# Mixture of experts in a hybrid decoder step: every low weight part is made by VectorE

## The chip, the cores and the metric

The kernel runs on one core of a Trainium2 chip. The metric is the device time of one execution in microseconds (us); the time given is the median of three runs. The engines go by the profile's names: PE is TensorE (PEld its weight loads), DVE is VectorE, ACT is ScalarE, POOL is GpSimd, SP is SyncE, which here only issues DMAs.

## The reference

One inference step of a two-layer decoder for 256 prompt positions and 64 sample positions (320 tokens of width 1024). Layer 0 is pooling and forgetting attention, cross-attention and a dense SwiGLU; layer 1 is a convolution module and stick-breaking attention, cross-attention and a mixture of eight experts. Only the last part is touched here:

```
logits = (h @ w_router).astype(f32) + b_router
top_val, top_idx = lax.top_k(logits, 2)
gates = softmax(top_val)              # spread over the 8 experts: combine
for e in range(8):
    out = out + combine[..., e:e+1] * swiglu(h, we_gate[e], we_up[e], we_down[e])
# swiglu(h, g, u, d) = (silu(h @ g) * (h @ u)) @ d,  1024 -> 3584 -> 1024, all fp32
```

## The kernel before

Each expert handles up to 128 gathered tokens. Its weights stream from HBM in 42 pieces of 128x2048 fp32 (1 MB). Seven column blocks (STAGES) of 512 hidden channels give the products (0, j) gate, (1, j) up and (2, j) down, j from 0 to 6. PRODUCTS (line 61) is the order of their use: (0,0), (1,0), then for j from 1 to 6 the three (0,j), (1,j), (2,j-1), and last (2,6). Each product takes two pieces, q = 0 and q = 1.

TensorE multiplies in a rounded fp32 form, so that each fp32 operand is split in a high and a low part, and three products of parts are summed (split_product, line 1072): high by high, low tokens by high weight, high tokens by low weight. A piece costs 12 matmuls of 128x512. For each piece:

- SP loads it into one of seven raw buffers (PRING = 7) as soon as TensorE has finished the piece seven places earlier (line 1380).
- ACT copies it to its high part (weights_hi, line 2147; the copy helper records line 1672).
- The low part, raw minus high, is written over the raw buffer. VectorE makes it for 35 of the 42 pieces (weights_lo, line 2858); GpSimd for the seven with m = 2 and q = 1, the second piece of every down product (POOLED, line 65; pooled, line 1601). Each has a semaphore of its own, and lo_parts (line 393) names the one and the count that TensorE waits for before a piece.

Each engine runs its own queue in order. VectorE's is written in expert (line 2867): at product b it makes the low parts of product b + 2, and beside that hidden(j), which multiplies the gate by the up result (line 2874), hidden_lo(j), the low part of the transposed hidden block (line 2879), and tokens_lo (line 2864), the low part of the next expert's tokens. At a product (0, j) the order is: low parts of (2, j-1), then hidden_lo(j-1). At (1, 6) it is: low parts of (2, 6), hidden(6), tokens_lo of the next expert; then follow the first piece of the next expert, hidden_lo(6), and the second piece.

TensorE transposes the hidden block j (line 1140) after product (0, j+1), multiplies (1, j+1), and then needs hidden_lo(j) for (2, j). At an expert's end it transposes the next expert's tokens (line 1118).

The results of the first seven experts go to scratch memory, the last one from expert 6 by a DMA that SP issues before piece 12 of expert 7 (line 1368). In the last expert, GpSimd's queue fetches them back per token in six indirect DMAs (outputs_back, line 1629), the first after that store has landed, those from the third on after VectorE has used up the buffer two back. VectorE adds them to x in combine(0) to combine(5) (line 2849), at the products b = 7, 9, 11, 13, 15, 17 of the last expert. In GpSimd's queue these fetches stand between its low parts: two pieces, fetches 0 and 1, two pieces, fetches 2 and 3, one piece, fetches 4 and 5, two pieces.

Of the kernel before, what the change touches and what calls it, by code (L numbers as in the profile page):

```python
# [18 lines left out]
F32 = mybir.dt.float32  # L19
# [3 lines left out]
ALU = mybir.AluOpType  # L23
# [16 lines left out]
NE = 8  # L40
# [21 lines left out]
PIECES = [(m, j, q) for m, j in PRODUCTS for q in range(2)]  # L62
NPIECE = len(PIECES)
PIECE = SLOT // 2
POOLED = [i for i, (m, j, q) in enumerate(PIECES) if m == 2 and q == 1]
PRING = 7
CAP = P
ROUNDS = -(-T // CAP)
# [109 lines left out]
def decoder_step(nc, a, o, scratch, known):  # L178

    ctx = ExitStack()  # L180
    with ctx:
# [16 lines left out]
        def sem(name):  # L198
            return ctx.enter_context(nc.semaphore(name))
# [142 lines left out]
        def pieces_of(small, large):  # L342
            return [(small if s < RING else large)[:, (s % RING if s < RING else s - RING) * SLOT + q * PIECE:][:, 0:PIECE]
                    for s in (0, 1, 3, 4, 5, 6, 2) for q in range(2)]

        raw = pieces_of(small_ring, big)[:PRING]
        low = pieces_of(ring_r, big_r)[:PRING]
        high = pieces_of(ring_r, big_r)[PRING:]
# [14 lines left out]
        full = [sem(f"bank{b}_full") for b in range(8)]  # L363
        free = [sem(f"bank{b}_free") for b in range(8)]
        raw_full = [sem(f"raw{s}_full") for s in range(PRING)]
        moe_hi, moe_lo, moe_lo_pool, moe_used, moe_xhi, moe_hThi = (sem("moe_" + n) for n in (
            "weights_hi", "weights_lo", "weights_lo_pool", "weights_used", "tokens_hi", "hiddenT_hi"))
        slot_full = [sem(f"slot{s}_full") for s in range(XSLOTS)]
        knat_full = [sem(f"knat{s}_full") for s in range(4)]
        ffn_gate, ffn_up, ffn_silu, ffn_h, ffn_down, ffn_whi, ffn_wlo, ffn_hsplit, ffn_hlo_ready = (  # L370
# [15 lines left out]
        def primed(s, value):  # L386

            return s, value + 1
# [3 lines left out]

        def lo_parts(n, i):

            mine = i % NPIECE in POOLED
            rank = sum((p_ in POOLED) == mine for p_ in range(i % NPIECE))
            per = len(POOLED) if mine else NPIECE - len(POOLED)
            return moe_lo_pool if mine else moe_lo, n * per + (i // NPIECE * per + rank + 1)

        def used(n, m, j):  # L400

# [37 lines left out]

        stream = list(w_stream())  # L440
        place = {key: (n % RING, n // RING) for n, (key, _) in enumerate(stream)}

        FBLK = DFF // 256
        n0 = next(n for n, (key, _) in enumerate(stream) if key[1] == 1)
        extra = [0, 2 * (FBLK // 2 + 1), 2 * (FBLK // 2)]

# [3 lines left out]
        def slot_of(key):  # L450

            s, use = place[key]
            n = next(m for m, (k, _) in enumerate(stream) if k == key)
            return s, use + 1 + (extra[s] if n >= n0 else 0)
# [37 lines left out]
        def _(pe):  # L492
# [581 lines left out]
            def split_product(n, m, j, out, x_hi_lo, chunks, between=None):  # L1074


                for q in range(2):
                    i = 2 * PRODUCTS.index((m, j)) + q
                    pe.wait_ge(*lo_parts(n, i))
                    w = [t[i % PRING].rearrange("p (k n) -> p k n", k=chunks) for t in (high, low)]  # L1080
                    for k in range(chunks):
                        kk = q * chunks + k
                        for xa, wa in ((0, 0), (1, 0), (0, 1)):
                            for dst, wcols in out(w[wa][:, k, :]):
                                ins = mm(dst, x_hi_lo[xa][kk], wcols,  # L1085
                                         start=(m < 2 or j == 0) and kk == 0 and (xa, wa) == (0, 0),
                                         stop=(m < 2 or j == STAGES - 1) and kk == 2 * chunks - 1 and wa == 1)
                    ins.then_inc(moe_used, 1)
                    if q == 0 and between is not None:
                        between()  # L1090
# [320 lines left out]
        def _(pool):  # L1411
            tt, ts = nc.gpsimd.tensor_tensor, nc.gpsimd.tensor_scalar
# [116 lines left out]
            r = NSAMP  # L1529
# [65 lines left out]
                        pool.dma_start(new_rows("sb_v", t), v[0:ROWS[t], t, :]).then_inc(*sets("v_out", 1, by=16))  # L1595
                    state_stores(1, "conv", CBUF, "state_conv")

            def pooled(n, pieces):
                for i in pieces:
                    pool.wait_ge(moe_hi, n * NPIECE + (i + 1))  # L1600
                    tt(low[i % PRING], raw[i % PRING], high[i % PRING].bitcast(F32), ALU.subtract) \  # L1601
                        .then_inc(moe_lo_pool, 1)

            def send_rows(r):

                pool.wait_ge(moe_rows_at, r + 1)
                if type(r) is int:
                    pool.wait_ge(moe_fill, 16)
                else:
                    pool.wait_ge(moe_rows_in, r * 16 * (NE - 1))  # L1610
                    pool.sem_inc(pool_passed, 1)
                for i in range(6):
                    t = i // 2
                    pool.indirect_dma_start(
                        out=scratch["tokens"], out_offset=bass.IndirectOffsetOnAxis(ap=row_at[0:ROWS[t], i:i + 1], axis=0),
                        in_=h[0:ROWS[t], t, :], in_offset=None, bounds_check=NE * CAP - 1, oob_is_err=False) \
                        .then_inc(moe_sent, 16)

            def outputs_back(r, i):

                t = i // 2
                if i == 0:
                    pool.wait_ge(*primed(moe_y_out, (r + 1) * 16 * (NE - 1)))
                    pool.wait_ge(*primed(moe_gathered, (r + 1) * 2 * NE))
                if i >= 2:
                    pool.wait_ge(*primed(moe_combined, r * 6 + (i - 1)))
                if type(r) is not int:
                    pool.sem_inc(pool_passed, 1)
                pool.indirect_dma_start(
                    out=moe_back[i % 2][0:ROWS[t], :], out_offset=None, in_=scratch["outputs"],  # L1630
                    in_offset=bass.IndirectOffsetOnAxis(ap=row_at[0:ROWS[t], i:i + 1], axis=0),
                    bounds_check=(NE - 1) * CAP - 1, oob_is_err=False).then_inc(moe_back_in[i % 2], 16)

            def expert_round(r):
                send_rows(r)
                with pool.Fori(0, NE - 1) as e:
                    pooled(e + r * NE, POOLED)
                n = r * NE + (NE - 1)
                pooled(n, POOLED[0:2])
                outputs_back(r, 0)  # L1640
                outputs_back(r, 1)
                pooled(n, POOLED[2:4])
                outputs_back(r, 2)
                outputs_back(r, 3)
                pooled(n, POOLED[4:5])
                outputs_back(r, 4)
                outputs_back(r, 5)
                pooled(n, POOLED[5:])

            expert_round(0)  # L1650
            pool.wait_ge(*at("cmax"))
            most = pool.value_load(cmax_i[0:1, 0:1])
            with pool.If(most > CAP):
                with pool.Fori(1, ROUNDS) as r:
                    expert_round(r)
# [556 lines left out]
        def _(dve):  # L2212
# [347 lines left out]
            for t in range(TILES):  # L2560
                r = ROWS[t]
                ins = V.tensor_tensor(lf_y[0:r, t, :], bank[b][0:r, 16 * t:16 * t + 8], b_f[0:r, :], ALU.add)
            step(ins)
            for t in range(TILES):
                r = ROWS[t]
# [191 lines left out]
            for t in range(TILES):  # L2757
                r = ROWS[t]
# [24 lines left out]
            for t in range(TILES):  # L2783
                r = ROWS[t]
# [67 lines left out]
            def weights_lo(n, b, parts=(0, 1)):  # L2852

                for i in (2 * b + q for q in parts):
                    if i % NPIECE in POOLED:
                        continue
                    dve.wait_ge(moe_hi, n * NPIECE + (i + 1))
                    V.tensor_tensor(low[i % PRING], raw[i % PRING], high[i % PRING].bitcast(F32), ALU.subtract) \  # L2858
                        .then_inc(moe_lo, 1)
# [107 lines left out]
```

## Time and profile before

| | us |
|---|---|
| median of three runs | 2050.26 (2046.18 to 2051.13) |
| the profiled execution | 2052.65 |
| its span in the profile | 2050.8 |
| before the experts' first product | about 1064 |
| experts and end | 1064 to 2051 |

The profile is of one execution. Times in the views count from the span's start; what lies around the span is 1.85 us. A timeline row has the start, the duration, the engine, the line, the operation with output and inputs, the count, and in brackets how long the engine stood idle before it and what released it. PE's matmuls are pipelined: a row's duration is longer than the step from one start to the next.

### The profile page before, as it was taken

To read this page: it belongs to the slowest core of one execution; us is meant where nothing else is said; L and a number is where in the kernel's file an instruction comes from. 1 tells how busy PE (TensorE), PEld (TensorE's weight loads), DVE (VectorE), ACT (ScalarE), POOL (GpSimd) and SP (SyncE) were. 2 spreads that over 40 slices of the span, in tenths; PEclk is the share of its full clock that TensorE was granted. 3 is DMA by queue.
4 is the path that set the end of the run, shared out by engine and by line. 5 is a ranking of instruction groups with operands and counts; after the bars stand their busy time and mean duration, and the time that the engine had idled before them with its cause. 6 is when DMAs were issued, how large, how long until landed. Compare 5 with 4: busy or idle time off the path is not lost.

```text
span 2050.8 us, 23715 instructions
## 1 busy us (share of the span) xinstructions
PE 1851.5 (90%) x8761; PEld 1449.0 (71%) x8761; DVE 1266.6 (62%) x1170; ACT 1064.8 (52%) x1052; POOL 460.6 (22%) x225
## 2 busy tenths in 40 slices
PE   6998978899998845697789999999999999999987
PEld 5785343799987834434378888888888888888865
DVE  5543032544435996203158888787878878788875
ACT  4333122423224315602137777777777777777663
POOL 4220010000003740001013322322332232233243
PEclk9999999899998976899969999999999999999999
DMA  9443206454444520421629999999999999999984
GB/s 302 137 157 107 94 29 207 144 162 126 150 142 166 192 81 26 149 82 41 215 96 381 373 374 388 363 393 361 390 374 377 387 364 394 363 389 372 374 334 151
DMA packets 236737, 497.88 MB, mean 243 GB/s; under 512 B 14994, under 2 KB 46882, under 8 KB 236653
## 3 DMA queue, kind: packets, MB, share of 16 engines
q1 hardware_dynamic: 223629, 479.11, 65.2%
q0 software_dynamic: 4544, 13.57, 1.9%
q10 hardware_dynamic: 8496, 4.33, 0.7%
q8 instruction: 39, 0.64, 0.1%
q14 instruction: 29, 0.24, 0.0%
HBM read 480.46 MB, written 17.35 MB: 243 GB/s over the span
## 4 chain that ended last, share of the span: by engine, by line
PE 78%; DVE 11%; issue 4%; ACT 3%; DMA 2%; POOL 1%; SPq 1%; DVEq 0%; ACTq 0%; POOLq 0%
PE bank L1085 40%; PE bank L532 8%; PE bank L960 8%; DVE big L2718 4%; PE bank L569 4%; PE bank L980 3%; PE bank L567 2%; DVE small_ring_r L2858 1%; PE bank L596 1%; PE bank L1140 1%; ACT big_r L1672 1%; PE bank L720 1%; PE bank L1106 1%; DMA small_ring<-in_w_ck 1%; PE bank L522 1%
## 5 line engine op out<-in xcount | busy, mean ns | idle before, releaser
L1672 ACT ACTIVATE big_r<-small_ring 128x2048 fp32r<-128x2048 f32 x240 | 456.0, 1915 | 139.3 <-DMA small_ring<-in_we_up 45.7
L2858 DVE TENSOR_TENSOR small_ring_r<-small_ring,big_r 128x2048 fp32r<-128x2048 f32 x168 | 441.2, 2656 | 44.5 <-ACT big_r L1672 44.4
L1085 PE MATMUL bank<-big_r,hT_r 128*128 128x512 f32 x1024 | 385.9, 395 | 10.3 <-DVE small_ring_r L2858 8.7
L1085 PE MATMUL bank<-small_ring_r,hT_r 128*128 128x512 f32 x768 | 302.3, 394 | 0.0
L1085 PE MATMUL bank<-big_r,kM_r 128*128 128x512 f32 x704 | 275.8, 392 | 0.0
L1085 PEld LDWEIGHTS bank<-big_r,hT_r 128*128 128x128 f32 x1024 | 193.3, 189 | 50.8 <-issue 11.2
L1672 ACT ACTIVATE small_ring_r<-big 128x2048 fp32r<-128x2048 f32 x96 | 183.3, 1916 | 52.2 <-DMA big<-in_we_up 28.0
L1601 POOL TENSOR_TENSOR small_ring_r<-small_ring,big_r 128x2048 fp32r<-128x2048 f32 x24 | 124.6, 5193 | 374.5 <-ACT big_r L1672 374.5
L2858 DVE TENSOR_TENSOR big_r<-big,small_ring_r 128x2048 fp32r<-128x2048 f32 x72 | 176.1, 2461 | 26.9 <-ACT small_ring_r L1672 26.9
L1601 POOL TENSOR_TENSOR big_r<-big,small_ring_r 128x2048 fp32r<-128x2048 f32 x24 | 123.4, 5141 | 197.8 <-ACT small_ring_r L1672 197.8
L1085 PEld LDWEIGHTS bank<-small_ring_r,hT_r 128*128 128x128 f32 x768 | 145.1, 189 | 30.2
L1085 PEld LDWEIGHTS bank<-big_r,kM_r 128*128 128x128 f32 x704 | 133.2, 189 | 26.8
L1672 ACT ACTIVATE big_r<-big 128x2048 fp32r<-128x2048 f32 x59 | 113.2, 1918 | 41.6 <-DMA big<-in_we_up 12.8
L532 PE MATMUL bank<-small_ring,h 128*128 128x512 f32 (+1 forms) x288 | 128.6, 604 | 2.9 <-ACT h L1672 2.1
L960 PE MATMUL bank<-hT_r,big_r 128*128 128x320 f32 x352 | 110.1, 313 | 5.2 <-DVE small_ring_r L2636 5.2
L1085 PE MATMUL bank<-big_r,PT_r 128*128 128x512 f32 x416 | 112.9, 390 | 0.4 <-DVE PT_r L2879 0.4
L2347 DVE TENSOR_TENSOR x<-x,bank 128x512 f32<-128x512 f32 (+1 forms) x24 | 16.4, 685 | 155.8 <-PE bank L532 155.8
L960 PE MATMUL bank<-hT_r,small_ring_r 128*128 128x320 f32 x352 | 109.9, 312 | 0.0
L2858 DVE TENSOR_TENSOR big_r<-big,big_r 128x2048 fp32r<-128x2048 f32 x40 | 91.4, 2285 | 27.9 <-ACT big_r L1672 27.9
L532 PEld LDWEIGHTS bank<-small_ring,h 128*128 128x128 f32 (+1 forms) x288 | 49.3, 176 | 80.0 <-issue 80.0
L1085 PE MATMUL bank<-small_ring_r,PT_r 128*128 128x512 f32 x352 | 98.9, 392 | 3.4 <-DVE PT_r L2879 3.4
L1085 PE MATMUL bank<-big_r,kN_r 128*128 128x512 f32 x352 | 96.0, 395 | 0.0
(398 smaller groups left out, 3252.7 us busy)
## 6 DMA issues: line engine op xcount, KB each, us to landing
small_ring<-in_we_gate SPq DMA_DIRECT2D x80, 1024.0 KB, 5.9
small_ring<-in_we_up SPq DMA_DIRECT2D x64, 1024.0 KB, 5.4
big<-in_we_down SPq DMA_DIRECT2D x64, 1024.0 KB, 5.8
big<-in_we_up SPq DMA_DIRECT2D x48, 1024.0 KB, 6.6
small_ring<-in_we_down SPq DMA_DIRECT2D x48, 1024.0 KB, 5.7
big<-in_we_gate SPq DMA_DIRECT2D x32, 1024.0 KB, 5.2
small_ring<-in_w_gate SPq DMA_DIRECT2D x11, 1024.0 KB, 5.5
small_ring<-in_w_up SPq DMA_DIRECT2D x11, 1024.0 KB, 8.0
```

The costliest lines, as they stand in the source:

```text
L522: ins = tr(bank[b][:, k * P:k * P + ROWS[t]], src[0:ROWS[t], t, (4 * kh + k) * P:(4 * kh + k + 1) * P], ident[0:ROWS[t], 0:ROWS[t]])
L532: ins = mm(bank[b][0:ROWS[t], 0:cols], xT[:, k, t0:t0 + ROWS[t]], w[:, k, col0:col0 + cols], start=k == 0, stop=k == nk - 1)
L567: ins = mm(bank[b][:, 0:T], w[wa][:, k, i * P:(i + 1) * P], x[xa][kk], start=first, stop=last)
L569: ins = mm(bank[b][0:ROWS[i], :], x[xa][kk][:, i * P:i * P + ROWS[i]], w[wa][:, k, :], start=first, stop=last)
L596: ins = tr(bank[b][:, c * P:(c + 1) * P], knat[:, j % 4, c * P:(c + 1) * P], ident)
L960: ins = mm(bank[bk][:, 0:T], w[wa][:, m, k, f2 * P:(f2 + 1) * P], ffn_x[:, k, :] if xa == 0 else ffn_xlo[k // 4][:, k % 4, :], start=k == ...
L980: ins = mm(out[0:ROWS[t], :], (ffn_hhi, ffn_plo)[xa][f2][:, t * P:t * P + ROWS[t]], w[wa][:, f2, wc], start=first and (xa, wa) == (0, 0), ...
L1085: ins = mm(dst, x_hi_lo[xa][kk], wcols, start=(m < 2 or j == 0) and kk == 0 and (xa, wa) == (0, 0), stop=(m < 2 or j == STAGES - 1) and kk ...
L1601: tt(low[i % PRING], raw[i % PRING], high[i % PRING].bitcast(F32), ALU.subtract) \
L1672: return A(out, in_, ACT.Copy)
L2718: ins = V.scalar_tensor_tensor(accp, inp, cw[:, j, c:c + 1], accp, ALU.mult, ALU.add)
L2858: V.tensor_tensor(low[i % PRING], raw[i % PRING], high[i % PRING].bitcast(F32), ALU.subtract) \
```

## The change

POOLED and GpSimd's pooled are removed, together with the semaphore moe_lo_pool. VectorE's weights_lo no longer leaves out the seven pieces, so that it makes all 42 of an expert in the order of PRODUCTS; lo_parts counts them all on one semaphore. GpSimd keeps the sending of the token rows at the start and the six fetches of the last expert, now one behind the other with nothing between. What the pieces are split into, the order of the products, the DMAs of SP and ACT's queue stay.

```diff
-POOLED = [i for i, (m, j, q) in enumerate(PIECES) if m == 2 and q == 1]
...
         def lo_parts(n, i):
-            mine = i % NPIECE in POOLED
-            rank = sum((p_ in POOLED) == mine for p_ in range(i % NPIECE))
-            per = len(POOLED) if mine else NPIECE - len(POOLED)
-            return moe_lo_pool if mine else moe_lo, n * per + (i // NPIECE * per + rank + 1)
+            return moe_lo, n * NPIECE + (i + 1)
...
-            def pooled(n, pieces):
-                for i in pieces:
-                    pool.wait_ge(moe_hi, n * NPIECE + (i + 1))
-                    tt(low[i % PRING], raw[i % PRING], high[i % PRING].bitcast(F32), ALU.subtract) \
-                        .then_inc(moe_lo_pool, 1)
...
             def expert_round(r):
                 send_rows(r)
-                with pool.Fori(0, NE - 1) as e:
-                    pooled(e + r * NE, POOLED)
-                n = r * NE + (NE - 1)
-                pooled(n, POOLED[0:2])
-                outputs_back(r, 0)
-                outputs_back(r, 1)
-                pooled(n, POOLED[2:4])
-                outputs_back(r, 2)
-                outputs_back(r, 3)
-                pooled(n, POOLED[4:5])
-                outputs_back(r, 4)
-                outputs_back(r, 5)
-                pooled(n, POOLED[5:])
+                for i in range(6):
+                    outputs_back(r, i)
...
             def weights_lo(n, b, parts=(0, 1)):
                 for i in (2 * b + q for q in parts):
-                    if i % NPIECE in POOLED:
-                        continue
                     dve.wait_ge(moe_hi, n * NPIECE + (i + 1))
                     V.tensor_tensor(low[i % PRING], raw[i % PRING], high[i % PRING].bitcast(F32), ALU.subtract) \
                         .then_inc(moe_lo, 1)
```

## Rows read from the trace of the kernel before

**Rows 1.** Windows: length, busy (count) of PE, PEld, DVE, ACT, POOL, clock, DMA share, GB/s.

```profile
1776.57:1895.98 119.41, 118.84 (x540) 98.14 (x541) 99.23 (x52) 91.34 (x63) 35.60 (x7) 1.00 1.02 378
1895.98:2028.36 132.38, 121.85 (x536) 98.81 (x536) 106.86 (x58) 83.14 (x56) 51.43 (x13) 0.97 0.88 325
...
1960.00:1970.00 10.00, 10.00 (x47) 7.98 (x46) 10.00 (x6) 7.11 (x5) 0.84 (x1) 1.00 1.04 398
```

**Rows 2.** Waits from 1240 to 1950 us: total us, times, longest us.

```profile
PEld bank L1085 <- DVE small_ring_r L2858: 5.3, 6, 1.1
...
PE bank L1085 <- DVE PT_r L2879: 2.8, 6, 0.7
```

**Rows 3.** Timeline of POOL, DVE and PE at the last expert's long stall.

```profile
1971.96 6.11 POOL L1601 TENSOR_TENSOR big_r<-big,small_ring_r 128x2048 fp32r<-128x2048 f32 x1 [11.13 <-ACT small_ring_r L1672]
1978.22 1.01 POOL L1629 DMA_INDIRECT gain<-scratch_outputs,row_at  x1
...
1985.41 1.28 DVE L2849 SCALAR_TENSOR_TENSOR x<-gain,rt,x 128x1024 f32<-128x1024 f32 x1 [11.22 <-DMA gain<-scratch_outputs,row_at]
...
1989.04 0.76 PE L1085 MATMUL bank<-big_r,hT_r 128*128 128x512 f32 x1 [7.90 <-DVE small_ring_r L2858]
1989.60 0.63 PE L1085 MATMUL bank<-big_r,kM_r 128*128 128x512 f32 x1
```

**Rows 4.** VectorE's low-part line, largest group: minimum, median, maximum in ns.

```profile
L2858 DVE TENSOR_TENSOR small_ring_r<-small_ring,big_r x168: 2273/2281/6085, 1047.5 to 2014.4; 128x2048 fp32r<-128x2048 f32 x168
```

**Rows 5.** Timeline of POOL, DVE and PE about one product (2, 0).

```profile
1320.56 6.33 POOL L1601 TENSOR_TENSOR small_ring_r<-small_ring,big_r 128x2048 fp32r<-128x2048 f32 x1 [24.04 <-ACT big_r L1672]
...
1320.11 2.29 DVE L2858 TENSOR_TENSOR small_ring_r<-small_ring,big_r 128x2048 fp32r<-128x2048 f32 x1
1322.61 0.69 DVE L2879 TENSOR_TENSOR PT_r<-bank,PT_r 128x512 fp32r<-128x512 f32 x1 [0.22 <-ACT PT_r L1672]
1324.42 4.62 DVE L2858 TENSOR_TENSOR small_ring_r<-small_ring,big_r 128x2048 fp32r<-128x2048 f32 x1 [1.11 <-ACT big_r L1672]
...
1327.18 1.07 PE L1085 MATMUL bank<-big_r,PT_r 128*128 128x512 f32 x4
```

**Rows 6.** Timeline of POOL, DVE, ACT and PE at an expert's end.

```profile
1768.31 5.38 POOL L1601 TENSOR_TENSOR big_r<-big,small_ring_r 128x2048 fp32r<-128x2048 f32 x1 [1.24 <-ACT small_ring_r L1672]
...
1766.46 2.76 DVE L2858 TENSOR_TENSOR big_r<-big,small_ring_r 128x2048 fp32r<-128x2048 f32 x1 [1.11 <-ACT small_ring_r L1672]
1769.60 0.69 DVE L2874 TENSOR_TENSOR qz<-Pr,bank 128x512 f32<-128x512 f32 x1 [0.38 <-PE bank L1085]
1770.51 1.29 DVE L2864 TENSOR_TENSOR kM_r<-bank,hT_r 128x512 fp32r<-128x512 f32 x2 [0.22 <-ACT hT_r L1672]
1772.80 3.04 DVE L2858 TENSOR_TENSOR small_ring_r<-small_ring,big_r 128x2048 fp32r<-128x2048 f32 x1 [1.01 <-ACT big_r L1672]
1775.77 0.68 DVE L2879 TENSOR_TENSOR PT_r<-bank,PT_r 128x512 fp32r<-128x512 f32 x1
1776.37 6.68 DVE L2858 TENSOR_TENSOR small_ring_r<-small_ring,big_r 128x2048 fp32r<-128x2048 f32 x3
...
1764.52 3.71 ACT L1672 ACTIVATE small_ring_r<-big 128x2048 fp32r<-128x2048 f32 x2
...
1772.88 0.60 PE L1140 MATMUL bank<-consts,qz 128*128 128x128 f32 x4
1776.57 1.19 PE L1085 MATMUL bank<-small_ring_r,PT_r 128*128 128x512 f32 x4 [0.32 <-DVE PT_r L2879]
```

**Rows 7.** Timeline of SP and DVE: the store before the fetches, the first combine.

```profile
1915.83 0.42 SPq L1368 DMA_DIRECT2D scratch_outputs<-qz  x1
...
1952.86 1.28 DVE L2849 SCALAR_TENSOR_TENSOR x<-gain,rt,x 128x1024 f32<-128x1024 f32 x1 [0.35 <-DMA gain<-scratch_outputs,row_at]
```

**Rows 8.** DMA from 1900 us on: a queue's packets, MB, share; issues, KB, us to landing.

```profile
q0 software_dynamic: 736, 2.24, 4.0%
...
scratch_outputs<-qz SPq DMA_DIRECT2D x1, 512.0 KB, 9.8
```

More of the change, by code:

```diff
@@ L365, in decoder_step @@
         raw_full = [sem(f"raw{s}_full") for s in range(PRING)]
-        moe_hi, moe_lo, moe_lo_pool, moe_used, moe_xhi, moe_hThi = (sem("moe_" + n) for n in (
-            "weights_hi", "weights_lo", "weights_lo_pool", "weights_used", "tokens_hi", "hiddenT_hi"))
+        moe_hi, moe_lo, moe_used, moe_xhi, moe_hThi = (sem("moe_" + n) for n in (
+            "weights_hi", "weights_lo", "weights_used", "tokens_hi", "hiddenT_hi"))
         slot_full = [sem(f"slot{s}_full") for s in range(XSLOTS)]
```

## The prediction

> **What bounds the kernel now.** I read the windows by stage first, then the waits, then the timelines where PE stands still.
>
> From 1064 us on the kernel is eight equal experts. One of them takes 119.41 us, and PE is busy for 118.84 of them, with a DMA share of 1.02 and 378 GB/s [rows 1]. The waits say that PE is the bound and not the DMAs: over six experts PE's matmuls waited 2.8 us for hidden_lo, and its weight loads 5.3 us for the low part made just before it, both once per expert, at its end [rows 2]. VectorE is busy for 99.23 us of the 119.41, POOL for 35.60.
>
> The last expert is the exception. It has four matmuls fewer (536 to 540) and takes 132.38 us [rows 1]: 13 us more than its neighbour. The reader is to see why [rows 3]. POOL made a low part at 1971.96, for which it had waited 11.13 us, and only behind it issued the third fetch, at 1978.22. VectorE's combine(2) needs that fetch and stood idle for 11.22 us until 1985.41; the low parts behind combine(2) came late, and PE stood idle for 7.90 us until 1989.04. The next matmul comes 0.56 us later [rows 3], where the mean step of an expert is 119.41 / 540 = 0.22, and the granted clock of this expert is 0.97 on the mean, of the one before 1.00 [rows 1]: after the stall PE ran for a while on the lower of its levels, 1.2 GHz.
>
> **The change part by part.**
>
> VectorE's added work. A low part on VectorE takes 2.28 us in the median but up to 6.09 [rows 4]. The long ones stand beside POOL's: POOL's piece of 1320.56 ends at 1326.89, and VectorE's piece of 1324.42 ends at 1329.04, 2.15 later; POOL's piece of 1768.31 ends at 1773.69, and VectorE's of 1772.80 ends at 1775.84, again 2.15 later [rows 5, 6]. So VectorE's instruction with two operands in SBUF waits until POOL's is done, and loses that with the change. In a row of three undisturbed ones the step is (6.68 - 2.28) / 2 = 2.20 us [rows 6]. An expert then costs VectorE 42 x 2.20 = 92.4 us, and the 16 short instructions (7 hidden, 7 hidden_lo, 2 tokens_lo) 16 x 0.6 = 9.6: 102 us of the 119.4, hardly more than the 99.23 of now. That is the lower end. The upper is that a piece keeps its present mean for some other reason: (99.23 - 9.6) / 36 = 2.49 us [rows 1], and 42 x 2.49 + 9.6 = 114 us. Either end is under 119.4; I take 102, since the median is the undisturbed piece.
>
> Where the seven pieces stand. Six per expert come before hidden_lo(j-1). The tightest is the first: VectorE's piece of 1320.11 is done, by the step, at 1322.3; the added one (its high part is there, POOL began on it at 1320.56) at 1324.5, and hidden_lo, now at 1322.61, at 1325.2. PE needs it at 1327.18 [rows 5]: 2.0 us to spare, and the piece after it, now ending at 1329.04, is done at 1327.4. They fall into VectorE's waits for ACT. So the steady stage stays PE's, and I cost these six at nothing; without this cover each us past the spare would cost 8 us over the eight experts.
>
> The seventh stands at the expert's end, before hidden(6) and tokens_lo. High parts come from ACT at 1766.4 and 1768.23; the low parts are then made at 1766.46 and 1768.7, hidden(6) at 1770.9 in place of 1769.60, tokens_lo at 1771.5 to 1772.8, just ahead of PE's transposes at 1772.88. The next expert's first piece starts at 1772.80 as now, but is done at 1775.0 in place of 1775.84, and hidden_lo(6) at 1775.7 in place of 1776.45: the 0.32 us that PE waited before 1776.57 are gone, with some 0.1 us to spare [rows 6]. At best the seven boundaries give back what the weight loads waited, 7 x 5.3 / 6 = 6.2 us; by the matmuls' wait it is 7 x 2.8 / 6 = 3.3 us [rows 2]; at worst hidden(6) comes late to the transposes and costs as much. I take half of the middle one, 1.6 us, since the margins are of 0.1 us.
>
> POOL's queue in the last expert. The fetches no longer stand behind low parts. The store of expert 6 is issued at 1915.83 and lands 9.8 us later [rows 7, 8], so that fetches 0 and 1 can leave at 1926 in place of 1943. Combine(0), which now starts at 1952.86 after a wait of 0.35 [rows 7], no longer waits. Fetch 2 waits for combine(0) alone, so it leaves at about 1954 and is there some 7 us later (1978.22 to 1985.41 now [rows 3]), long before combine(2), which began its wait at 1985.41 - 11.22 = 1974.2 [rows 3]. The 11.22 us of VectorE and PE's 7.90 go, and the slow matmuls after it. What is late next is nothing on VectorE: the six combines of 1.28 us [rows 7] add under 8 us in the last expert, and selecting the gates (line 2838) some 4: 114 of 119. The last expert should take what the one before takes, less the four transposes it lacks (0.4): 119.0 us. Gain 132.38 - 119.0 = 13.4 us. The boundaries are counted above.
>
> What is left against this is the DMAs. With 42 x 1.05 = 44.0 MB of weights, the store's 0.5 and the fetches' 2.24 MB [rows 8] the last expert moves 46.8 MB, against 45.1 in one before it (weights, one store, one fetch of tokens of 0.5 each). In the best window, 398 GB/s flowed [rows 1]: 46.8 MB / 398 = 117.6 us, just inside 119.0. The fetches now come right behind the store. I take off 1 us, with 0 and 5 as bounds.
>
> Sum: 13.4 + 1.6 - 1 = 14.0 us. From the profiled execution 2052.65 - 14.0 = 2038.6 us. That execution lies 2.4 us above the median of 2050.26, so I forecast 2036 us.
>
> **The rivals.**
>
> The DMAs are the bound as soon as the stall is gone. For it: a share of 1.02 in the steady stage, at 378 GB/s [rows 1]. Then the last expert takes 46.8 MB / 378 = 123.8 us, the boundaries give nothing, and the gain is 8.6 us: 2042 us. Against it: windows at 398, and PE, not the loads, has the last word. In its strongest form the last expert's 132.38 us are already those of its loads, and only the 1.6 us of the boundaries come: 2048.7 us; against that stand its 398 GB/s in a window, more than a whole stall-free expert needs, and a rate over all of it of 325 [rows 1], which is what a queue that waits for PE gives. A rule of the Trainium skill speaks for this form: SBUF — State Buffer, section "Summary: rules for kernel authors", says to reckon with about 358 GB/s between HBM and SBUF, by which 46.8 MB would take an estimated 131 us and the time would stay near 2049 us. By that rule the 378 GB/s over a whole expert [rows 1] could not be; the trace disagrees on this core.
>
> The stall only moves: the third fetch or a low part is late for another reason in the last expert, and only the shorter pieces help. For it: VectorE has 5 us to spare there, and no order of the fetches without POOL's pieces is in the trace. It leaves 8 of the 13.4 us standing: 2050.3 - 14 + 8 = 2044 us.
>
> Slower: the added piece delays hidden_lo. Its place is the product (2, j) in all experts. The spare there is 2.0 us, in the one place worked out above; if all 48 (six per expert) are like it, a piece of more than 4.2 us makes PE wait, and one of 4.5 us eats the whole gain (48 x 0.3 = 14 us). At 4.62 us, which VectorE's piece of 1324.42 took [rows 5], the loss is 48 x 0.4 = 19 us: 2036 + 19 = 2055 us. Against it: the long durations are those beside POOL, of which none are left.
>
> That the change doesn't do what it says can hardly be: no other work of POOL remains in the stage but the fetches.
>
> **How the numbers follow.** Forecast 0.70; DMAs at 378 GB/s 0.14, and in their strongest form 0.04; the stall moves 0.07; slower 0.05. Faster by over 0.3% means under 2044.1 us, about what a measurement here can tell: the forecast, the DMAs at 378, and a part of the moved stall, 0.86. Within 0.3%: 0.08. Slower 0.06. The range goes from 2028 (the middle gain at all boundaries, no loss to DMAs, 2033, and the 5 us by which the runs before differ) to 2047, which takes in the DMA rival and the moved stall.
>
> **What would show it.** POOL's busy time in an expert falls from 35.60 to nothing; VectorE's low parts all lie near 2.28 us, 42 an expert, and its busy time in an expert is about 102 us. PE takes some 119 us for each expert, the last one too, with no wait near 7.90 us and a clock of 1.00 throughout; fetch 0 leaves before 1930, and no combine waits for a fetch. The forecast is wrong if low parts over 3 us remain with POOL at rest, if PE waits for hidden_lo in the middle of an expert, or if PE waits for loads in the last one.

## The result

The changed kernel takes 2037.35 us, the median of eight runs (2030.33 to 2040.26); the kernel before, measured beside it, 2050.73 (2046.18 to 2056.99). The ratio is 0.9928, with an interval of 0.9909 to 0.9947: faster by 0.7%. Two later sets with the same kernel gave 0.9957 (0.9941 to 0.9974) and 0.9956 (0.9938 to 0.9974). By the medians the three sets gained 13.4, 8.8 and 9.3 us, so that the gain is some 10 us and the first set is the most favourable of the three.

The profiled executions can't simply be subtracted. The new one has a span of 2032.2 us, 18.6 less than before, but 8.5 us of that lie ahead of the experts, in code that is the same: the first product starts at 1055.84 in place of 1064.35 us. Over all the profiles of this study it starts between 1053 and 1064 us, whatever the kernel. So I take the time from the first product to the span's end: 986.4 us before, 976.4 after, 10.1 less. (Before stands on one profile, the change on three.) The first products, before and after:

```profile
1064.35 0.79 PE L1085 MATMUL bank<-big_r,hT_r 128*128 128x512 f32 x1 [1.59 <-DVE kM_r L2864]
```

```profile
1055.84 0.79 PE L1081 MATMUL bank<-big_r,hT_r 128*128 128x512 f32 x1 [1.59 <-DVE kM_r L2841]
```

The windows of the kernel after, of an inner expert and of the last, with the columns as in [rows 1]: length, busy us and count of PE, PEld, DVE, ACT and POOL, clock, DMA share, GB/s. (They begin 0.1 to 0.2 us behind the product's first matmul, which shortens a length by up to 0.1.)

```profile
1766.00:1884.50 118.50, 118.50 (x541) 98.12 (x541) 104.55 (x59) 91.25 (x63) 0.00 (x0) 1.00 1.03 381
1884.50:2009.88 125.38, 119.30 (x537) 97.26 (x536) 108.79 (x65) 83.78 (x56) 11.51 (x6) 1.00 0.94 345
```

An inner expert has fallen from 119.41 to 118.50, and PE is busy all the time. The last one has fallen from 132.38 to 125.38 us, and is still 7 us longer than its neighbour. POOL is at rest but for the fetches.

VectorE's low parts (minimum, median, maximum in ns; before: [rows 4]):

```profile
L2835 DVE TENSOR_TENSOR small_ring_r<-small_ring,big_r x192: 2274/2291/2296, 1039.0 to 1994.9; 128x2048 fp32r<-128x2048 f32 x192
L2835 DVE TENSOR_TENSOR big_r<-big,small_ring_r x96: 2276/2293/2296, 1064.0 to 2003.7; 128x2048 fp32r<-128x2048 f32 x96
```

All 336 lie between 2.27 and 2.30 us; before, the longest took 6.09.

About the product (2, 0), where [rows 5] gave the spare, the timeline of DVE and PE has

```profile
1309.83 4.49 DVE L2835 TENSOR_TENSOR small_ring_r<-small_ring,big_r 128x2048 fp32r<-128x2048 f32 x2
1314.23 0.68 DVE L2856 TENSOR_TENSOR PT_r<-bank,PT_r 128x512 fp32r<-128x512 f32 x1
1314.84 2.28 DVE L2835 TENSOR_TENSOR small_ring_r<-small_ring,big_r 128x2048 fp32r<-128x2048 f32 x1
...
1316.92 1.07 PE L1081 MATMUL bank<-big_r,PT_r 128*128 128x512 f32 x4
```

The added piece is the second of the x2. hidden_lo is done at 1314.91, 2.0 us before PE's need, and the next piece follows without the long wait for POOL. At the expert's end, where [rows 6] stood before:

```profile
1756.19 4.49 DVE L2835 TENSOR_TENSOR big_r<-big,small_ring_r 128x2048 fp32r<-128x2048 f32 x2 [1.11 <-ACT small_ring_r L1651]
1760.60 0.68 DVE L2851 TENSOR_TENSOR qz<-Pr,bank 128x512 f32<-128x512 f32 x1
1761.20 1.28 DVE L2841 TENSOR_TENSOR kM_r<-bank,hT_r 128x512 fp32r<-128x512 f32 x2
1762.53 2.29 DVE L2835 TENSOR_TENSOR small_ring_r<-small_ring,big_r 128x2048 fp32r<-128x2048 f32 x1
1764.74 0.69 DVE L2856 TENSOR_TENSOR PT_r<-bank,PT_r 128x512 fp32r<-128x512 f32 x1
...
1762.62 0.60 PE L1136 MATMUL bank<-consts,qz 128*128 128x128 f32 x4
...
1765.82 1.07 PE L1081 MATMUL bank<-small_ring_r,PT_r 128*128 128x512 f32 x4
```

tokens_lo ends at 1762.48, 0.14 us before the transposes at 1762.62; hidden_lo(6) ends at 1765.43, and PE goes on at 1765.82 with no idle time. Here the margins of a tenth or two held.

In the last expert PE still waits, in three rows of the waits from 1884.5 us on (total, times, longest):

```profile
PE bank L1136 <- DVE qz L2851: 3.2, 1, 3.2
PE bank L1081 <- DVE kN_r L2856: 1.6, 2, 1.0
PE bank L1081 <- DVE PT_r L2856: 1.4, 1, 1.4
```

All name VectorE, but what made VectorE late is mostly not its own. The chain that ended last goes, for the earliest of them (PE at 1930.64, behind hidden_lo in kN_r), back to a load that took 10.76 us to land, issued between the first two fetches:

```profile
1914.96 10.76 DMA small_ring<-in_we_down
1925.74 1.93 ACT big_r L1651
1927.69 2.29 DVE small_ring_r L2835
1929.99 0.61 DVE kN_r L2856
...
1930.64 11.22 PE bank L1081 x48
```

For the longest, the 3.2 us before the transposes at the expert's end, the chain goes back to a load too, but it also passes a combine, which is VectorE's own work:

```profile
1985.78 9.73 DMA big<-in_we_down
...
1995.53 1.93 ACT big_r L1651
...
2000.38 1.19 DVE x L2828
...
2005.97 0.61 DVE qz L2851
...
2006.62 0.66 PE bank L1136 x4
```

The fetches stand in POOL's timeline at

```profile
1913.76 3.09 POOL L1619 DMA_INDIRECT gain<-scratch_outputs,row_at  x1 [860.67 <-DMA scratch_outputs<-qz]
...
1942.60 2.27 POOL L1619 DMA_INDIRECT gain<-scratch_outputs,row_at  x1 [24.44 <-DVE x L2828]
```

that is, right behind the store's landing and behind combine(0); no combine waits for a fetch any more, where combine(2) had waited 11.22 us [rows 3].

### The profile page after: what moved, and what is told of

The parts are those of the page before. It is cut to its first block, busy times and chain, and to the rows that moved or that the text cites. A ratio compares the mean times of both kernels' runs of the same rounds, so it can differ in the third digit from the quotient of the medians.

```text
span 2032.2 us, 23749 instructions
## 1 busy us (share of the span) xinstructions
PE 1839.1 (90%) x8761; PEld 1442.1 (71%) x8761; DVE 1313.8 (65%) x1226; ACT 1064.9 (52%) x1052; POOL 173.7 (9%) x169
## 4 chain that ended last, share of the span: by engine, by line
PE 80%; DVE 10%; DMA 4%; ACT 2%; issue 2%; SPq 1%; POOL 0%; DVEq 0%; ACTq 0%
PE bank L1081 42%; PE bank L528 8%; PE bank L956 8%; DVE big L2697 4%; PE bank L565 4%; PE bank L976 3%; PE bank L563 2%; DMA big<-in_we_down 1%; PE bank L592 1%; PE bank L1136 1%; DMA small_ring<-in_we_down 1%; PE bank L716 1%; PE bank L1102 1%; DMA small_ring<-in_w_ck 1%; PE bank L518 1%
## 5 line engine op out<-in xcount | busy, mean ns | idle before, releaser
L2835 DVE TENSOR_TENSOR big_r<-big,small_ring_r 128x2048 fp32r<-128x2048 f32 x96 | 219.5, 2291 | 39.1 <-ACT small_ring_r L1651 39.0
L1651 ACT ACTIVATE big_r<-big 128x2048 fp32r<-128x2048 f32 x59 | 113.2, 1919 | 44.8 <-DMA big<-in_we_down 13.4
L2835 DVE TENSOR_TENSOR big_r<-big,big_r 128x2048 fp32r<-128x2048 f32 x48 | 109.9, 2290 | 36.1 <-ACT big_r L1651 36.1
L2603 DVE TENSOR_TENSOR L<-S,bank 128x320 f32<-128x320 f32 x22 | 10.7, 488 | 130.7 <-PE bank L956 130.7
L1081 PEld LDWEIGHTS bank<-big_r,PT_r 128*128 128x128 f32 x416 | 78.0, 188 | 17.9 <-DVE PT_r L2856 1.8
```

Of the source, the lines that this page charges most:

```text
L1081: ins = mm(dst, x_hi_lo[xa][kk], wcols, start=(m < 2 or j == 0) and kk == 0 and (xa, wa) == (0, 0), stop=(m < 2 or j == STAGES - 1) and kk ...
L1651: return A(out, in_, ACT.Copy)
```

## The experiments

Two questions: are the gains at the boundaries and in the last expert two things or one, and what keeps the last expert at 125 us? Each table row is one profiled execution; "stage" is from the first product to the span's end, "last" is the window from expert 6's last down product to that of expert 7 (to 0.2 us), "ratio" against the kernel before, timed beside it.

| kernel | stage | last | ratio (interval) |
|---|---|---|---|
| before | 986.4 | 132.4 | |
| the change | 976.4 | 125.4 | 0.9928 (0.9909 to 0.9947) |
| the change again, third | 976.2, 974.4 | 127.0, 124.8 | 0.9957, 0.9956 |
| in the last expert alone | 983.1 | 127.5 | 0.9963 (0.9947 to 0.9978) |
| in the first seven alone | 981.0 | 131.3 | 0.9955 (0.9938 to 0.9972) |
| fetches ahead, POOL's pieces kept | 983.3 | 128.7 | 0.9984 (0.9968 to 1.0001) |
| POOL with idle work | 1045.8 | | 1.0265 (1.0242 to 1.0287) |
| no fetch | 967.5 | 118.5 | 0.9924 (0.9903 to 0.9945) |
| no combine | 973.3 | 124.3 | 0.9948 (0.9930 to 0.9967) |
| spread, again | 972.6, 971.9 | 122.7, 121.3 | 0.9934, 0.9932 |
| late fetches | 970.2 | 118.2 | 0.9933 (0.9909 to 0.9958) |

**In the last expert alone.**

```diff
-                    if i % NPIECE in POOLED:
+                    second = i % NPIECE in POOLED
+                    if second and not last:
                         continue
...
-                        .then_inc(moe_lo, 1)
+                        .then_inc(moe_lo_pool if second else moe_lo, 1)
```

GpSimd's queue in the last expert is the six fetches.

> The kernel before, with the change made in the last expert alone: there VectorE makes all 42 low parts and GpSimd only fetches; in the first seven experts GpSimd keeps its pieces. My theory (two separate gains: a fetch that was stuck behind GpSimd's pieces in the last expert, and some 0.8 us per expert at the boundaries): the last expert falls from 132.4 to about 125.4 us as after the change, the others keep 119.3 with their wait for hidden_lo, and the time is about 7 us under the kernel before. Rival (the gain is one thing, GpSimd's instructions slowing VectorE everywhere): the last expert gains 2 us at most, and so does the time.

The last expert fell to 127.5, 4.9 us less and not 7; the inner ones stayed at 119.2 to 119.3 us, with one of 121.35. The median is 7.7 us under the kernel before. One extra long wait at a boundary spoils the size in this profile, at its end:

```profile
1772.24:1893.59 121.35, 118.86 (x541) 98.13 (x541) 101.00 (x52) 92.86 (x64) 34.65 (x7) 1.00 1.02 376
1893.59:2021.06 127.47, 122.52 (x535) 99.82 (x536) 108.83 (x65) 81.68 (x55) 13.60 (x6) 0.97 0.89 333
```

Behind that wait (2.5 us) and the later ones PE ran slower for a while: the mean granted clock of the second window is 0.97.

**In the first seven alone.** The converse (`if second and last: continue`; GpSimd's loop over the first seven experts is gone, its queue in the last one as before).

> The converse: VectorE makes all low parts in the first seven experts, GpSimd has its seven pieces and the fetches between them in the last one, as before. My theory: the first seven take 118.5 us each without a wait at the boundary (about 6 us in all), the last one stays near 132 with VectorE waiting some 11 us for the third fetch; the time is 4 to 6 us under the kernel before. Rival: the last expert's stall was built up by lateness from the experts before it; then it shrinks to 125 here too, and the time equals that of the full change.

As expected: the inner experts take 118.6 us, and the last one is nearly as long as before, with the same cause, a combine that waits 11.4 us for its fetch. An inner window and the last one:

```profile
1772.03:1890.66 118.63, 118.63 (x540) 98.29 (x541) 104.41 (x59) 91.07 (x63) 0.00 (x0) 1.00 1.02 378
1890.66:2021.98 131.32, 120.82 (x537) 98.55 (x535) 106.44 (x58) 84.01 (x56) 49.36 (x13) 0.97 0.89 330
```

The wait, from this kernel's waits of VectorE (total, times, longest):

```profile
DVE x L2847 <- DMA gain<-scratch_outputs,row_at: 11.4, 1, 11.4
```

So there are two gains, and by the stage they nearly add: 3.3 and 5.4 us by the two halves, 8.7 together, against 10.1 for the whole. The medians, 7.7 and 8.2 us under the kernel before, add to more than the whole gave in any of its three sets: they show that either half helps, and not how closely the two add.

**Fetches ahead.**

```diff
-                pooled(n, POOLED[0:2])
+                pooled(n, POOLED[0:1])
                 outputs_back(r, 0)
                 outputs_back(r, 1)
-                pooled(n, POOLED[2:4])
+                pooled(n, POOLED[1:2])
                 outputs_back(r, 2)
+                pooled(n, POOLED[2:3])
                 outputs_back(r, 3)
-                pooled(n, POOLED[4:5])
+                pooled(n, POOLED[3:4])
                 outputs_back(r, 4)
                 outputs_back(r, 5)
-                pooled(n, POOLED[5:])
+                pooled(n, POOLED[4:])
```

> The kernel before with one thing changed: in the last expert's queue of GpSimd each fetch stands before the piece that it need not wait for (one piece, fetches 0 and 1, one piece, fetch 2, one piece, fetch 3, one piece, fetches 4 and 5, three pieces). GpSimd still makes its seven pieces in all experts. My theory (the order alone makes the long stall): no combine waits for a fetch, PE's wait of 7.9 us is gone, and the last expert falls to 125 to 128 us, short of the full change only by what the long VectorE pieces cost; the time is 4 to 7 us under the kernel before. Rival (VectorE's long pieces beside GpSimd's make the stall): the last expert stays above 130, and the time within 2 us of the kernel before.

Neither held. No combine waits for a fetch, but the last expert takes 128.7 us and the time falls by 2 us, hardly more than can be told. The waits of its last expert:

```profile
PE bank L1085 <- DVE kN_r L2880: 3.4, 1, 3.4
...
PE bank L1085 <- POOL small_ring_r L1601: 1.5, 1, 1.5
```

The first stands behind a VectorE piece that took 6.70 us beside POOL's, the second is POOL's own piece, late behind a fetch. So the order alone, which made the 7.9 us of [rows 3], gives 3.1 of the 10.1 us of the stage; the rest goes only with the pieces themselves, which bring waits of their own.

**POOL with idle work.** The changed kernel; POOL subtracts a spent buffer from itself, and nobody waits for it.

```diff
+                    for half in range(2):
+                        pool.wait_ge(*primed(moe_idle, n * 2 * len(POOLED) + 2 * k + half))
+                        tt(vM_t[:, 0:1024], vM_t[:, 0:1024], vM_t[:, 0:1024], ALU.subtract).then_inc(moe_idle, 1)
```

> The changed kernel, with GpSimd given work that nobody waits for: at the places of its old pieces in the first seven experts it subtracts a spent buffer from itself (two instructions of 128x1024 for each old piece). My theory (GpSimd's reading instruction holds up VectorE's two-operand ones): VectorE's low parts lengthen again beside them, to 3 us and more, and the experts go from 118.5 towards 119.3 us, up to 5 us in all. Rival (what was saved at the boundaries is the wait for GpSimd's own results): VectorE's low parts stay at 2.29 us, the experts at 118.5 and the time at that of the changed kernel.

The sign was right and the size wrong by far: 55 us over the kernel before. An inner expert takes 128.34 us, by its window:

```profile
1444.70:1573.04 128.34, 122.62 (x542) 99.70 (x540) 122.63 (x59) 92.23 (x64) 48.40 (x14) 0.97 0.96 351
```

And from the timeline of VectorE and of POOL, a low part beside two idle pieces:

```profile
1501.92 3.98 DVE L2846 TENSOR_TENSOR small_ring_r<-small_ring,big_r 128x2048 fp32r<-128x2048 f32 x1
...
1500.18 7.48 POOL L1601 TENSOR_TENSOR vM<-vM 128x1024 f32<-128x1024 f32 x2 [9.73 <-ACT big_r L1662]
```

VectorE's low parts beside POOL's work take up to 3.98 us again, and their mean is 2.65 (43 in 114.05 us). VectorE and PE are now busy equally long, 122.6 of the 128.34 us, and in the chain that ended last VectorE's low parts have 41.5% of this window, PE's matmuls of products 10.6%. With all 42 pieces VectorE can't bear this much of POOL's work beside it. The idle work is more than the old pieces were (48.40 us busy an expert, against 35.60 [rows 1]), so it shows that POOL's work holds up VectorE though nobody waits for it, and not what the old pieces would cost beside 42. POOL is held up as well: its idle pieces take 1.92 us at the shortest and 3.82 in the median.

**No fetch, no combine.** Two kernels that leave the first seven experts' outputs out of the sum. In the first, `pool.sem_inc(moe_back_in[i % 2], 16)` stands for the fetch; in the second, `dve.sem_inc(moe_combined, 1)` for the combine.

> The changed kernel without the six fetches of the last expert: their semaphores are raised without a transfer, and the six combines add what lies in the buffers, so that the first seven experts' outputs are left out of the sum. The question is what keeps the last expert at 125.4 us where the others take 118.5. Theory D (2.24 MB of fetches crowd the weight loads, which land late): without them the last expert falls to 119 to 120 us, the loads there land in 6 to 7 us as elsewhere instead of 9, and the time falls by about 6 us under the changed kernel. Theory V (VectorE's six combines and gates fill its queue): it stays at 124 us or more.

> The changed kernel with the six fetches but without the six combines: VectorE waits for each fetch and raises the semaphore, and adds nothing, so that the first seven experts' outputs are left out of the sum. Theory D (the fetches crowd the loads): the last expert stays within 2 us of 125.4. Theory V (VectorE's queue): it falls to 119 to 121 us.

The first takes 118.51 us for the last expert, as for any other, the second 124.30:

```profile
1889.22:2007.73 118.51, 118.38 (x537) 97.50 (x535) 108.11 (x65) 83.99 (x56) 0.00 (x0) 1.00 0.93 346
```

```profile
1886.97:2011.27 124.30, 119.39 (x537) 97.17 (x535) 102.02 (x59) 83.71 (x56) 11.80 (x6) 1.00 0.95 348
```

It is the transfers, and hardly VectorE's work: without the combines, PE's wait at the expert's end is still 2.0 us of the 3.2, and the last expert takes only 0.5 us less than the shortest of the changed kernel's three (124.8). The landing times of the loads in the last expert say how (KB, us from issue to landing): with fetches, in the changed kernel, then without.

```profile
big<-in_we_down SPq DMA_DIRECT2D x8, 1024.0 KB, 9.7
```

```profile
big<-in_we_down SPq DMA_DIRECT2D x8, 1024.0 KB, 5.7
```

These are the loads that differ most; over the six groups of loads the medians are 5.3 to 9.7 us with fetches and 5.1 to 7.5 without, and single ones, as that in the first chain above, take over 10. A load is issued when its buffer comes free, seven pieces ahead of its use, some 19 us. When it lands 4 us later, the spare of VectorE's queue is gone, and hidden_lo or hidden, which stand behind that piece, are late for PE. (The fetches are shown to be the cause; that a deeper ring would hide the late landing was not tried.)

Whether the loads land late because the fetches' bytes fill the DMAs or because each load is held up some other way, the runs do not separate. As an estimate, 2.24 MB of fetches at the 398 GB/s of the best window [rows 1] take 5.6 us, near the 6.9 us that the fetches cost. But a rate of 398 GB/s is not enough to make loads late: the changed kernel shows it beside the first two fetches and also in an inner expert, whose loads land in 5.1 to 6.5 us (medians of the groups):

```profile
1913.00:1930.00 17.00, 16.68 (x76) 13.26 (x74) 12.07 (x7) 10.60 (x8) 4.10 (x2) 1.00 1.04 398
1790.00:1810.00 20.00, 20.00 (x92) 16.55 (x91) 18.45 (x11) 14.68 (x10) 0.00 (x0) 1.00 1.04 398
```

**Spread.** Combines at the products 7, 10, 13, 16, 19 and 20, and fetch i behind combine i-1 (4 and 5 both behind combine 3).

```diff
-                if i >= 2:
-                    pool.wait_ge(*primed(moe_combined, r * 6 + (i - 1)))
+                if i:
+                    pool.wait_ge(*primed(moe_combined, r * 6 + min(i, 4)))
```

> The changed kernel with the fetches spread: combines at the products 7, 10, 13, 16, 19, 20 instead of 7 to 17 in steps of two, and a fetch leaves only behind the combine before it, fetches 4 and 5 behind combine 3. So fetch 1 no longer comes right behind the store and fetch 0, one combine falls to each round of three products, and the last two fetches come when the weights are all but loaded. If theory D or theory V holds, the last expert falls from 125.4 to 120 to 122 us and the time by 3 to 5 us under the changed kernel; if the stalls come from elsewhere, it stays at 125.

> The spread fetches a second time, beside the changed kernel on the same chip: by the first run's profile its last expert is 3 to 4 us shorter than that of the changed kernel (122.7), and the time should be 3 to 4 us less.

122.7 and 121.3 us for the last expert; the medians lie 4.5 and 6.3 us under that of the changed kernel beside them. Fetches and combines both moved, so that this run does not tell the two apart.

**The change again.**

> The changed kernel once more, as the reference for the others on this chip: 2037 us, 118.5 us per expert, 125 for the last. If the 120.7 us that the fourth expert took in its first profile were of that execution alone, all of the first seven take 118.5 here; if they belong to the kernel, the fourth is long again.

> The changed kernel a third time, as the reference of this chip: 118.5 us for each of the first seven experts, 125 to 127 for the last, 2037 to 2041 us.

The fourth expert, of 120.72 us in the first profile, took 118.6 in both: that was of one execution. In the first profile its chain goes back to a late load, though no fetch runs there, and PE waits twice:

```profile
1438.48 9.80 DMA small_ring<-in_we_down
```

```profile
PE bank L1081 <- DVE kN_r L2856: 0.9, 1, 0.9
PE bank L1136 <- DVE kM_r L2841: 0.7, 1, 0.7
```

So loads can land late without the fetches; why they did there stays open. The medians were 2041.59 and 2038.65.

**Late fetches.** Each pair of fetches goes into a raw buffer of its own, once PE has used the last piece in it, and the six combines stand at the end of VectorE's queue.

```diff
+                if i % 2 == 0:
+                    pool.wait_ge(*primed(moe_used, (r + 1) * NE * NPIECE - PRING + (i // 2 + 1)))
...
+                    if last and b == len(PRODUCTS) - 1:
+                        for i in range(6):
+                            combine(r, i)
```

> The changed kernel with the six fetches moved behind the weight loads: each pair goes into a raw buffer of its own, as soon as TensorE has used the last piece in it (some 16, 13 and 11 us before the expert's end, when no load is left to issue), and all six combines stand at the end of VectorE's queue, where it waits for TensorE's last product. Theory D (only the fetches crowd the loads): the last expert takes 118.5 to 120 us, and the time is 5 to 7 us under the changed kernel, about 2031, unless the combines outlast the last product: then the end after it grows by 1 to 3 us. Rival (the last loads and VectorE's last pieces are late by themselves): 122 us or more for the last expert.

```profile
1892.83:2010.98 118.15, 118.15 (x536) 97.57 (x535) 103.39 (x60) 83.89 (x56) 8.37 (x6) 1.00 0.99 363
```

PE doesn't wait at all in the last expert, and the end after it is as long as before (22.3 us). By the stage, 970.2 us, this is the best of the kernels that do the whole sum; its median, 2035.62, lies 3.0 us under the changed kernel's beside it, less than the 5 to 7 expected, and two intervals of 0.2% each don't tell 3 us apart. In its own profile the second and the third of the first seven experts took 119.6 and 120.5 us, some 3 us over the others.

## Why the prediction was right

The time, 2037.35, lies 1.35 us from the forecast of 2036. Point by point it is less good: two terms were off, in opposite directions, and the nearness is partly luck. From the first product on, the change gave 10.1, 10.2 and 12.0 us in its three profiles, against the 14.0 of the forecast; the first set's 13.4 holds 3 us more than its own profile shows there, and the later sets gave 8.8 and 9.3.

- VectorE's added work: right. An inner expert has VectorE busy for 104.55 us (102 forecast), and all low parts take 2.29 us. The places of the seven pieces came out near those computed. For hidden_lo(6) the prediction's 0.1 us to spare was too little by its own times (done 0.75 us earlier, against a wait of 0.32), and it had 0.39.
- The boundaries: too small. I took 1.6 us, half of what the matmuls had waited. The first seven experts together took 831.6 us before, and 828.5, 826.7 and 826.9 in the three profiles of the change: 3.1, 4.9 and 4.8 us, the first of them with the long fourth expert. About the full price of the matmuls' wait, 3.3 us, or more came back, and not half of it. I halved it since the margins were thin. In the second and third profile they held at every boundary; in the first, tokens_lo was late once, at the end of the fourth expert (PE's 0.7 us for kM_r above).
- The last expert: too large. The fetch's stall of 11.22 us went, with PE's 7.90 and the slow matmuls behind it, and I forecast 13.4 less 1 for the DMAs. It gave 7.0, 5.4 and 7.6 us in three profiles. The step that failed is the allowance for the DMAs, "1 us, with 0 and 5 as bounds": it is 6.9 us (125.4 against 118.5 without fetches), outside its bounds. By two of the prediction's own signs it was wrong here: PE waited for hidden_lo in the middle of the last expert (at 1930.64), and behind late loads. I had reasoned with the throughput of a whole expert, 46.8 MB at 398 GB/s. The 46.8 MB were wrong: the last expert loads no first pieces of a next one, so that its window moves 43 MB (345 GB/s over 125.38 us; before, 325 over 132.38 [rows 1]). What the traces show is the landing time of loads, in the group that differs most 9.7 in place of 5.7 us, against a ring of seven pieces.
- The rival of the DMAs, at 0.14, priced the last expert at 123.8 us, nearest of all (124.8 to 127.0), but by luck: with 43 MB its rule gives 114 us, no bound at all. And the inner experts gained too, at 381 GB/s, more than the 378 that it took for the limit, so that the rate is not the bound there.
- The moved stall was half right: a new wait, of 3.2 us, stands at the expert's end. The slower rival did not come: hidden_lo had its 2.0 us to spare in the inner expert shown. But longer VectorE pieces do make PE wait, as the idle work on POOL shows.

The wait of VectorE's two-operand instructions for POOL's is what the Trainium skill says in SBUF — State Buffer, section "Who interferes with whom": such an instruction contends with a GpSimd instruction that reads SBUF, by an exclusive lock. The traces agree: the pieces ended 2.15 us after POOL's in [rows 5, 6], and took up to 3.98 in place of 2.28 us beside POOL's idle work. The rate of 358 GB/s that the Trainium skill gives there (section "Summary: rules for kernel authors"), which spoke against the change, is contradicted by this trace: 381 GB/s over a whole expert.

## What to carry to other kernels

Work given to GpSimd is not free for VectorE even where nobody waits for its results: count what it adds to every two-operand instruction beside it, and look at what its queue holds back (here, fetches). When a stall goes, look for the transfers that run beside the streaming loads, and ask for the landing time of a load against the depth of the ring, not only for the mean rate. Extra transfers are better off where the stream has ended, as the one profile of the late fetches shows (118.2 us in place of 125).

## What was not expected

- The time ahead of the experts varies by 11 us (first product from 1053 to 1064 us) in unchanged code, about as much as the change gives; the parts had to be compared from the first product on.
- POOL's idle work, two instructions of 128x1024 seven times an expert, 48 us busy of 128, cost 10 us per expert, far above the 0.9 us by which an inner expert with POOL's pieces had been longer.
